# A hybrid trunk layer: the order of modulation products, token turnings and GpSimd's loads at its start

## What is computed

```python
mod = (jax.nn.silu(cond) @ w_mod + b_mod)[:, None, :]
sh1, sc1, g1, sh2, sc2, g2 = jnp.split(mod, 6, axis=-1)
h = rms_norm(x, norm1_w) * (1.0 + sc1) + sh1
...
qa, ka, va, qb, kb, vb, zb, a_f, a_b, b_f, b_b, ga, gb = jnp.split(h @ w_in, _in_split_points(), axis=-1)
qa = rms_norm(qa.reshape(B, L, H_A, D_HA), q_norm_w)
ka = rms_norm(ka.reshape(B, L, H_A, D_HA), k_norm_w)
```

## Time and profile before

| | us |
|---|---|
| median of 3 runs | 1249.64 |
| lowest and highest | 1248.31, 1255.67 |
| profiled execution, its own time | 1249.9 |
| its span | 1248.1 |
| TensorE busy in the span | 1116.6 (89%) |
| VectorE, ScalarE, GpSimd busy | 448.6, 332.6, 168.5 |
| bytes moved | 199.99 MB, 160 GB/s on average |
| mean granted clock of TensorE | 0.955 of full speed |

### The profile page before, as it was taken

How to read it: one execution, slowest core, us unless ns; L and a number is a source line. 1 busy time by engine, 2 the same in 40 slices (tenths; PEclk the granted TensorE clock), 3 DMA queues, 4 the chain that set the end, 5 groups by cost and what they waited for, 6 DMA issues and landing times.

```text
span 1248.1 us, 15933 instructions
## 1 busy us (share of the span) xinstructions
PE 1116.6 (89%) x6262; PEld 595.0 (48%) x6262; DVE 448.6 (36%) x868; ACT 332.6 (27%) x656; POOL 168.5 (13%) x260
## 2 busy tenths in 40 slices
PE   2699999999998989989999999999469999999990
PEld 1244456666555689986444444444233333333320
DVE  1222126777775755645411101223511111111115
ACT  4112134556553343325220000111211111111111
POOL 0000020011000346751000000000111111111100
PEclk9799999999999899999999999999769999999995
DMA  8802233335110113102021111132438999999926
GB/s 334 370 1 76 93 118 144 143 145 203 68 68 27 40 24 108 25 5 93 23 116 67 68 68 67 68 152 101 169 102 303 374 377 390 391 379 382 374 96 257
DMA packets 44192, 199.99 MB, mean 160 GB/s; under 512 B 18320, under 2 KB 23904, under 8 KB 32080
## 3 DMA queue, kind: packets, MB, share of 16 engines
q1 hardware_dynamic: 28544, 142.56, 29.9%
q10 hardware_dynamic: 4608, 30.18, 6.5%
q0 software_dynamic: 10960, 26.17, 5.8%
HBM read 190.69 MB, written 22.87 MB: 171 GB/s over the span
## 4 chain that ended last, share of the span: by engine, by line
PE 74%; DVE 10%; DMA 8%; ACT 3%; issue 3%; POOL 2%; SPq 0%; DVEq 0%; POOLq 0%; ACTq 0%
PE bank L1672 24%; PE bank L2237 10%; PE bank L1777 7%; PE bank L2258 6%; DMA arena<-h_scratch,arena 4%; PE bank L2094 3%; PE bank L2092 3%; PE bank L2225 2%; PE bank L1936 2%; PE bank L1826 2%; PE bank L1630 1%; PE bank L1946 1%; DMA arena<-in_w_blocks 1%; PE bank L1645 1%; PE bank L1762 1%
## 5 line engine op out<-in xcount | busy, mean ns | idle before, releaser
L1672 PE MATMUL bank<-arena 128*128 128x512 f32 x704 | 309.3, 595 | 4.4 <-DVE arena L1125 3.5
L1672 PEld LDWEIGHTS bank<-arena 128*128 128x128 f32 x704 | 132.3, 190 | 165.7 <-issue 164.6
L2237 PE MATMUL bank<-arena 128*32 128x512 f32 x1536 | 172.1, 599 | 1.3 <-DVE arena L1585 1.3
L1777 PE MATMUL bank<-arena 128*128 128x320 f32 x384 | 119.7, 453 | 0.0
L2237 PEld LDWEIGHTS bank<-arena 128*32 128x32 f32 x1536 | 48.1, 110 | 107.8 <-issue 107.8
L2258 PE MATMUL bank<-arena 128*32 128x512 f32 x768 | 87.4, 595 | 0.8 <-ACT arena L1065 0.8
L1777 PEld LDWEIGHTS bank<-arena 128*128 128x128 f32 x384 | 69.5, 192 | 35.4 <-issue 10.8
L1598 DVE TENSOR_TENSOR arena<-arena,bank 128x256 f32<-128x256 f32 x24 | 10.1, 421 | 175.2 <-ACT arena L1059 175.2
L708 POOL DMA_INDIRECT y_scratch<-arena x24 | 24.4, 1016 | 248.1 <-DVE arena L1591 248.1
L1463 DVE TENSOR_TENSOR arena<-arena,bank 128x512 f32<-128x512 f32 x10 | 6.9, 687 | 135.8 <-PE bank L2094 135.8
L988 ACT ACTIVATE arena<-bank 128x512 f32<-128x512 f32 x20 | 11.9, 597 | 145.3 <-PE bank L1672 145.2
(11 more groups left out here) (297 smaller groups left out, 1478.1 us busy)
## 6 DMA issues: line engine op xcount, KB each, us to landing
arena<-in_w_up SPq DMA_DIRECT2D x32, 2048.0 KB, 15.5
arena<-in_w_blocks SPq DMA_DIRECT2D x27, 2048.0 KB
arena<-in_w_down ACTq DMA_DIRECT2D x28, 1024.0 KB, 8.6
arena<-y_scratch SPq DMA_DIRECT2D x10, 512.0 KB, 9.4
arena<-in_bias POOLq DMA_DIRECT2D x3, 1536.0 KB, 11.4
arena<-in_w_down SPq DMA_DIRECT2D x4, 1024.0 KB, 8.2
arena<-in_x SPq DMA_DIRECT2D x5, 512.0 KB, 9.0
gram_scratch<-arena SPq DMA_DIRECT2D x10, 256.0 KB, 2.5
```

Of the source, the lines that this page charges most:

```text
L1672: last = mm(bank, hT[:, k, tok0[i]:tok0[i] + P], w[:, k, :], start=(k == 0), stop=(k == KC - 1))
L1777: last = mm(banks[5 + half][:, 0:HTOK], w[:, k, :], hT[:, k, half * HTOK:(half + 1) * HTOK], start=(k == 0), stop=(k == KC - 1))
L2237: last = mm(banks[2 + e % 2][at, :], rowsT[e % 2][:, k, at], eup[expert % SLOTS_W][:, k, :], start=(k == 0), stop=(k == KC - 1))
```

## The change

On TensorE, product 0 of the modulation goes ahead of all turnings, and the other products and column sums are put between the turnings. ScalarE's copies follow the same order. The transposes of `kctx` and their copy go to projection product 8. GpSimd's four loads and the two of `bias` all wait until the first projection product is done. The first two projection products wait for the modulation of each k by itself.

```diff
--- before.py
+++ after.py
@@ -575,11 +575,11 @@
         @block.gpsimd
         def _(pool):
             step = stepper(pool, "pool_step", {})
+            pool.wait_ge(S["proj_mm"], 1)
             pool.dma_start(kctx, t["kctx"]).then_inc(S["kv_ctx_in"], 16)
             pool.dma_start(vctx, t["vctx"]).then_inc(S["kv_ctx_in"], 16)
             pool.dma_start(conv_w, t["conv_w"].rearrange("p (a b) -> p a b", a=12)).then_inc(S["kv_ctx_in"], 16)
             pool.dma_start(w_ab, t["w_ab"].rearrange("p (a b) -> p a b", a=KC)).then_inc(S["kv_ctx_in"], 16)
-            pool.wait_ge(S["hT_ready"], 2 * T)
             for u in range(2):
                 pool.dma_start(bias[:, u], t["bias"][u].rearrange("p (h k) -> p h k", h=H_A)).then_inc(S[f"bias_in{u}"], 16)
 
@@ -760,12 +760,15 @@
             for i in range(T):
                 x_norm(i)
             step(sc.activation(stat[:, 0, :], stat[:, 0, :], ACT.Sqrt, bias=eps_col, scale=1.0 / D), "ssq_ready")
-            for i in range(T):
-                x_turned(i)
-            for j in range(4):
-                part_out(j)
-            act.wait_ge(S["kctxT_mm"], 1)
-            step(sc.activation(kctxT, banks[6][:, :].rearrange("p (a b) -> p a b", a=4), ACT.Copy))
+            part_out(0)
+            x_turned(0)
+            x_turned(1)
+            part_out(1)
+            x_turned(2)
+            x_turned(3)
+            part_out(2)
+            x_turned(4)
+            part_out(3)
             for u in range(2 * T):
                 act.wait_ge(S["proj_mm"], u + 1)
                 if u >= 2:
@@ -774,6 +777,9 @@
                 act.wait_ge(S["headsum"], u + 1)
                 step(sc.activation(headstat[:, u % 2, 8:16], headstat[:, u % 2, 0:8], ACT.Sqrt, bias=eps_col,
                                    scale=1.0 / D_HA), "headstd")
+                if u == 8:
+                    act.wait_ge(S["kctxT_mm"], 1)
+                    step(sc.activation(kctxT, banks[6][:, :].rearrange("p (a b) -> p a b", a=4), ACT.Copy))
                 if u >= 1:
                     v = u - 1
                     act.wait_ge(S["qkT_mm"], v + 1)
@@ -1672,17 +1678,34 @@
                     last = mm(bank, hT[:, k, tok0[i]:tok0[i] + P], w[:, k, :], start=(k == 0), stop=(k == KC - 1))
                 return last
 
-            for i in range(T):
-                x_turn(i)
+            def kctx_turn():
+                pe.wait_ge(S["kv_ctx_in"], 64)
+                pe.wait_ge(S["part_ready"], 4)
+                for a in range(4):
+                    last = nc.tensor.transpose(banks[6][:, a * P:(a + 1) * P], kctx[:, a * P:(a + 1) * P], ident)
+                last.then_inc(S["kctxT_mm"], 1)
+
+            def first_rows(u):
+
+                w = ringv[:, w_slot("qa")]
+                for k in range(KC):
+                    pe.wait_ge(S["hT_mod"], u * KC + k + 1)
+                    last = mm(banks[u][:, :], hT[:, k, tok0[u]:tok0[u] + P], w[:, k, :], start=(k == 0), stop=(k == KC - 1))
+                return last
+
             mod_mm(0)
-            for j in range(1, 4):
-                mod_mm(j)
-                mod_cols(j - 1)
+            x_turn(0)
+            x_turn(1)
+            mod_mm(1)
+            mod_cols(0)
+            x_turn(2)
+            x_turn(3)
+            mod_cols(1)
+            mod_mm(2)
+            x_turn(4)
+            mod_cols(2)
+            mod_mm(3)
             mod_cols(3)
-            pe.wait_ge(S["kv_ctx_in"], 64)
-            for a in range(4):
-                last = nc.tensor.transpose(banks[6][:, a * P:(a + 1) * P], kctx[:, a * P:(a + 1) * P], ident)
-            last.then_inc(S["kctxT_mm"], 1)
 
             def qk_turn(v):
                 pe.wait_ge(S["qk_ready"], v + 1)
@@ -1705,9 +1728,9 @@
                         pe.wait_ge(S["qk_ready"], u - 3)
                     else:
                         pe.wait_ge(S["va_ready"], u - 3 - 2 * T)
-                if u < 2:
-                    pe.wait_ge(S["hT_mod"], (u + 1) * KC)
-                rows_mm(banks[u % 4][:, :], name, u % T).then_inc(S["proj_mm"], 1)
+                if u == 8:
+                    kctx_turn()
+                (first_rows(u) if u < 2 else rows_mm(banks[u % 4][:, :], name, u % T)).then_inc(S["proj_mm"], 1)
                 if 1 <= u <= 2 * T:
                     qk_turn(u - 1)
```

## The result

The changed kernel takes 1230.43 us (median of 4 runs, 1228.51 to 1232.77); the kernel before, run beside it, 1248.97 (4 runs, 1246.77 to 1255.67). The ratio is 0.9846, its 95% interval 0.9824 to 0.9868: faster by 1.5%, 18.5 us. The forecast was 1231.5, with a range of 1227 to 1240.

What follows compares the result with a forecast made beforehand. TensorE, holding 74% of the chain, was taken as the bound, with the early wait for mod3 on its path. Gains 16.7 + 2.1 - 0.5 = 18.3 us from 1249.9 gave 1231.6, written 1231.5; range 1227 to 1240.

Steps and rivals of the forecast that it cites:

- Where the end is bound: Whole program: TensorE holds 74% of the chain, so a microsecond less early waiting is one off the end.
- signs of being wrong: Trace: mod0 landing after 18, granted clock 0.50 behind 25 us, or a longer distance from first projection to end.
- x and `mod0`: Start: without GpSimd's first four loads x lands 1.7 us earlier, at 12.0; mod0 is in at 16.5.
- the rival that they land together: Start: engines mix mod0 to mod2, product 0 starts at 25.6, everything moves 9 us, 1240.5; chance 0.08.
- The schedule: Front of TensorE: first projection at 40.2 instead of 56.91, a gain of 16.7 us, bounds 12 and 17.7.
- 0.7 added for roughness and waits: Before the first projection: 0.7 us allowed for fourteen added waits and schedule roughness, moving its start to 40.2.
- low end of the range: Whole kernel: 17.7 + 2.1 with better overlapping front turnings (0.7 and 1.5 more), 1227.5, so 1227.
- The margins: Front transfers: mod3 needed at 34.6, there at 31; qa needed at 40, lands at 36.
- The clock: First sixteen projection matmuls: clock stays at 1.00, removing the slow start's 2.1 us; bound below, nothing.
- The cold-front rival: Modulation front: array stays cold, slow products and turnings, 2.1 not gained; costs 9.2 us, 1240.7; chance 0.07.
- Keys and loads: Ahead of projection product 8: kctx transposes add 0.5 us to a dense stretch; GpSimd's late loads are hidden.
- The slower rival: Product 8: TensorE stops for GpSimd's late loads; 82 us from issue would make it 1% slower (1262); chance 0.02.

Runs made afterwards that it cites:

- all fourteen traces: One profiled execution each of the kernel before, the changed kernel (profiled twice) and variants with parts moved or matmuls added; median times 1228.98 to 1248.97 us.
- second profile of the changed kernel: The changed kernel, unaltered, profiled again beside a candidate on the same chip; median 1230.21 us, ratio to before 0.9836.
- late bias: Kernel before with only GpSimd's two bias loads moved behind the first projection product, four small loads left at the start; 1240.65 us, ratio 0.9925.
- k by k: On its own: kernel before with only the first two projection products waiting for each k's modulation separately; 1244.97 us, ratio 0.9968.
- Order alone: Kernel before with only the new TensorE and ScalarE order; loads, kctx transposes and first projection's waits as before; 1234.53 us, ratio 0.9875.
- without k by k: Changed kernel with the first two projection products again waiting for all eight k; 1233.31 us, ratio to before 0.9880.

## Why the prediction was right

**Where the end is bound.** That a microsecond saved ahead of the projections is one saved at the end held in all fourteen traces: the rest of the program, 1079.8 to 1084.4 us from `w_ab` on, does not follow the start of the projection. One of the prediction's signs of being wrong did come in the first pair of profiles: from the first projection matmul to the end it was 1192.9 us where before it was 1191.2 and 1189.6 was forecast. 2.0 us of this lie behind `w_ab`, and in the second profile of the changed kernel the distance was 1190.2. So the spread between executions is enough to explain it, without a later wait.

**x and `mod0`.** The squares started at 11.92 (12.0 was forecast) and `mod0` let product 0 start at 16.88 (16.5). The blocks are served in order; the rival that they land together would have put product 0 at 25.6, and falls.

**The schedule.** It ran ahead of mine: turnings 0 and 1 done at 23.2 instead of 24.0, since the array was through with its slow time in product 0 and turning 0 took 1.16 instead of 2.0; product 3 at 33.07 instead of 34.6, since sums and copies overlap more; sums 3 done at 36.8 instead of 38.2; 1.27 from there to the projection (1.3). The 0.7 added for roughness and waits was not needed: with all fourteen waits the sixteen matmuls took 14.00 in the second execution. So this term was 18.8 instead of 16.7, mis-sized by 2.1 and above its bound of 17.7. (The low end of the range has a slip of its own: 1249.9 - (17.7 + 2.1 + 0.7 + 1.5 - 0.5) is 1228.4, not 1227.5. Nothing hangs on it.)

The margins were thinner than forecast. The prediction gave `mod3` and `qa` 3 to 4 us in hand. The four modulation blocks landed at 16.7, 21.6, 26.5 and 31.4, each 4.9 us behind the one before, and `qa` at 37.55; they were needed at 33.07 and 38.09, so 1.7 and 0.5 us were in hand.

**The clock.** This term was put at 2.1 in full and was 0.7 in the first profile (16.23 to 15.54), 2.2 in the second. The step that failed is the one from a longest gap of about 1.3 us to a clock that stays up: the gap was 1.27, and the clock fell to 0.50 at about 38 all the same. Ahead of it TensorE was busy for 2.05 of 4 us (34 to 38), half of that with sums of two columns; but in the second execution it was 2.12 of 4, and the clock stayed up. So why it fell stays open. The text had named 0.50 behind 25 us as a sign that it is wrong, and that sign came; it cost 1.4 us. The cold-front rival is another thing: products 1 to 3 took 1.93 each in the changed kernel, so the front was at full clock and the rival falls. By the rule weighed there (the Trainium skill, TensorE: Matmul & The Clock Gate, Part 4: PE-mode transpose) transposes don't bring the full clock; here the trace differs, since turnings alone went from 0.196 to 0.105 us for a weight load.

**Keys and loads.** The transposes of `kctx` cost 0.44 between two projections (97.38 to 97.82 and 98.26) where 0.5 was set. 18.8 + 0.7 - 0.4 = 19.1 is what the first `w_ab` matmul moved (166.9 to 147.8), so the sum closes there. Behind it this pair of profiles gives back 2.0, which is spread, and their spans differ by 17.1 us. The medians differ by 18.5 (16.5 to 22.0 by the interval), and 18.3 was forecast. That it came so close is in part luck: two errors of opposite sign, 2.1 too little and 1.4 too much, nearly cancel.

**What each part is worth.** On its own, order brings 14.2 us at the first projection, late bias 9.3, k by k 2.8; taken out of the whole, k by k costs 2.6 and the loads 1.6 to 2.3. Order and bias remove the same wait for `mod3`, so their parts don't add. Order alone takes most of it because it frees the slot 10 us sooner (22.4 instead of 32.8). The slower rival, late loads of GpSimd, was never near: they landed by 53 and were needed at 97.8.

## What to carry to other kernels

Where a ring of buffers has run dry, look for the consumer whose finishing frees the slot, and ask what stands ahead of it that it does not need: product 0 stood behind forty transposes for no reason of data, and moving it up moved a 2 MB transfer up. That pays only until the transfer meets the ones ahead of it in its queue: against bias late alone `mod3` was issued 11.7 us sooner (20.6 instead of 32.3) and landed 8.4 sooner (31.4 instead of 39.8), 4.9 us behind `mod2`. Two remedies for one wait don't add, so price each with the other in place. A microsecond of difference is read at a fixed point of the trace behind the change, not from medians that scatter by three, and a clock reading from one execution needs a second one of the same program.

## What the runs showed of the hardware

The granted clock can fall to 0.50 (1.2 GHz) with no idle time of TensorE above 1.3 us, after a stretch that was busy for 2.05 of 4 us, half of that with two-column sums; and the same program keeps 1.00 there in another execution. In the changed order the length of the last idle stretch, 1.27 us in the changed kernel, 3.47 with the order alone and 3.96 without k by k, made no difference to the price: 15.54, 15.55 and 15.63 us for the sixteen matmuls. It is not the length that sets the price: with 3.47 us of idle time in the old order the sixteen took 16.67 (bias late), since the slow stretch reached further into them. A 2 MB block took 7.5 us from issue to landing with nothing of other queues beside it, and 14.5 beside 3.1 MB of another queue.
